# A hybrid decoder's decay rows: spread to all partitions by a transfer from memory in place of a TensorE product

## The chip, the cores and the metric

The kernel runs on one core of one Trainium2 chip. The metric is the device time of one execution in microseconds (us). The core has TensorE (PE), VectorE (DVE), ScalarE (ACT), GpSimd (POOL) and SyncE (SP, which here only starts transfers), and 16 DMA engines.

## The reference, cut to what matters

Two layers of a decoder trunk on 512 tokens of 1,024 channels. Each layer runs a state-space mixer (Mamba-2) and a differential attention mixer side by side, merges them by gates, and adds a squared-ReLU MLP. The part around the change is the state-space mixer with 32 heads of width 64, in 4 groups of 8 heads, over 4 chunks of 128 tokens:

```python
a_step = (dt * a)                       # per token and head
a_cum = jnp.cumsum(a_step, axis=2)      # running sums within a chunk
seg = a_cum[:, :, :, None] - a_cum[:, :, None, :]
decay = jnp.exp(jnp.where(causal, seg, -jnp.inf))
cb = jnp.einsum("bclgn,bcsgn->bclsg", Cc, Bc)
y_diag = jnp.einsum("bclsgr,bcsgrp->bclgrp", cb[..., None] * decay, X)
chunk_decay = jnp.exp(a_cum[:, :, -1])
```

For each head and chunk the kernel needs a 128 x 128 matrix with differences of the running sums: one token index lies over the partitions, the other along the row. The sum of the row's token has to be the same on all 128 partitions.

## The kernel before

All large products (projections, MLP) are made of units of 1,024 x 256 weights. Each weight is split into a high part in fp32r (`w_hi`, written by ACT, L930) and the rest (`w_lo`, written by GpSimd, L1796), and each product is three: high by high, high by low, low by high (L553 to L555 with 512 tokens as columns; L576 to L578, `unit_tokens`, with 256 columns). Raw weights are loaded by SyncE (L434) into two slots; a load waits until GpSimd is done with the slot, a conversion until PE is done with it, PE until GpSimd has written the low part (`lo_ready`).

The order of everything else is written out in ticks, from -10 to 59 for the state-space part and its surroundings in each layer. In each tick PE first does 2 to 6 parts of the running projection (`fill`; `SSD_FILL`), and then the small products of the tick. All engines go through the same ticks, each in its own order, and meet at semaphores. For tick t in 0 to 31:

- PE: `spread(t + 2)` (L721) takes one column of the selection matrix `sel`, broadcast over 128 columns as the weights, against `acum`, 64 rows by 512 columns, and so puts the running sums of head t + 2 on all partitions of a PSUM bank (banks 2 and 3 in turn). `acum` and `sel` are fp32r with 64 rows, since each sum is kept as a high part (rows 0 to 31) and the rest (rows 32 to 63). Then `diagonal(t)` (L734) multiplies the four 128 x 128 matrices `seg` of head t with `xdt`, in plain f32: eight instructions of 64 columns. Its end raises `m_used`. After it come chunk states (L745), off-diagonal products (L750), C by B (L758) and transposes (L618), as the tick has them.
- ACT: `decay(t + 1)` waits for the bank and for `m_used` of head t - 1, since `seg` has two buffers. Four activations (L1033, one per chunk, 128x128) compute relu(token's sum - row's sum) from PSUM into `seg`; after a drain one activation (L1037) takes the exponential of all four in place. Then ACT copies transposes out of PSUM (L1043, L1047), converts weights (L930), and starts and ends convolutions (L1011, L1017).
- DVE: `masked(t + 1)` (L1471) multiplies `seg` with the masked C by B.
- POOL: low parts of weights, and once a group of heads the tiles `xdt`, `xd` and the skip term.

Ahead of that, at tick -6, DVE makes `acum` out of PE's running sums (`decays_of_rows`, L1427 on), and `dcd`, which holds the chunks' last sums on a diagonal. PE sums `dcd` over its rows with a column of ones at tick -4 (`chunk_ends`, L770). The ticks' 32 heads in two layers make 64 calls of `spread`, at ticks -2 to 29.

Of the kernel before, what the change touches and what calls it, by code (L numbers as in the profile page):

```python
# [13 lines left out]
P = 128  # L14
# [77 lines left out]
LATE = [(0, m) for m in range(18, 24)] + [(1, m) for m in range(ADA)]  # L92
N_FIRST, N_EARLY, N_LATE = len(FIRST), len(EARLY), len(LATE)
N_LATE_AO = 2
ADA_G2 = LATE.index((0, ADA - 1))
EARLY_BUFS = 3
EARLY_AT = [37 + c for c in range(7)] + [44 + c // 2 for c in range(4 * N_EARLY - 7)]
# [48 lines left out]

BANK_KEYS = [[], [], [], []]
for _tick in range(T_FIRST, T_ATT):
    if 0 <= _tick + 2 < T_POST:
        BANK_KEYS[2 + _tick % 2].append(("sp", _tick + 2))  # L150
    if 0 <= _tick < T_POST and _tick % 2 == 0:
        BANK_KEYS[1].append(("d", _tick // 2))
    if step_at_tick(_tick):
        BANK_KEYS[0].append(step_at_tick(_tick))
    for _b, _key in EXTRA.get(_tick, ()):
        BANK_KEYS[_b].append(_key)
# [53 lines left out]
def build(nc, stream, dtw, params, consts, ropes, xT, xsave, out):  # L210
    ctx = ExitStack()
    with ctx:
        at = [nc.sbuf_base + (-nc.sbuf_base) % 32]

        ctx.enter_context(nc.sbuf_tensor("arena", [P, 212000 // 4], F32))

        def place(name, shape, dt, offset):
            return nc.alloc_sbuf_tensor_at(name, shape, dt, offset=offset)

# [37 lines left out]

        b_tok = place("b_tok", [P, TB, STATE], F32, r_op)
        cbm = place("cbm", [P, TB, P], F32, r_op + T2)
        seg = place("seg", [P, 2, TB, P], F32, r_op + 2 * T2)  # L260
        xdt = place("xdt", [P, TB, GW], F32, r_op + 4 * T2)
        xd = place("xd", [P, TB - 1, GW], F32, r_op + 8 * T2)
        state = place("state", [P, 2, GW], F32, r_op + 11 * T2)
        y_off = place("y_off", [P, GW], F32, r_op + 13 * T2)
        dcd = place("dcd", [2 * HEADS, HEADS, TB], F32R, r_op + 14 * T2)


        conv = place("conv", [P, 4, S], F32, r_g)
# [47 lines left out]
        def small(name, cols, dt=F32, rows=P):  # L316
            return place(name, [rows, cols], dt, region(cols * 4))
# [11 lines left out]
        lamw = small("lamw", 2 * AD)  # L329
        odd = small("odd", 8)  # L330
        lams, a_neg, subg = odd[:, 0:4], odd[:, 4:6], odd[:, 6:7]
        acum = small("acum", S, F32R, 2 * HEADS)
        sel = small("sel", HEADS + 2, F32R, 2 * HEADS)
        tok = place("tok", [P, TB, 3 * HEADS], F32, region(TB * 3 * HEADS * 4))
        ea_tok = place("ea_tok", [P, TB, HEADS], F32, region(TB * HEADS * 4))
        cdec = place("cdec", [P, HEADS, TB], F32, region(HEADS * TB * 4))
# [27 lines left out]
        con_in, par_in, dtw_in, x_in = sem("con_in"), sem("par_in"), sem("dtw_in"), sem("x_in")  # L364
        x_saved, x_back, rope_in, out_done = sem("x_saved"), sem("x_back"), sem("rope_in"), sem("out_done")
        ready = sem("ready")
        c_tanh, sel_ready = sem("c_tanh"), sem("sel_ready")
        S_ = {name: sem("s_" + name) for name in TOTAL if not name.startswith("bank")}

        LO_CREDIT, DONE_CREDIT, BANK_CREDIT, AUX_CREDIT, LAYER_CREDIT = 0, 4, 2, 1, 1  # L370
# [150 lines left out]
        def pe_program(pe):  # L521
# [115 lines left out]
            for l in range(DEPTH):  # L637
# [5 lines left out]
                if l == 0:  # L643
                    for n in range(2):
                        pe.wait_ge(pe_in[n], 16)
                        ada_piece(ada_pe[n], ab[3], 2 * FIRST_PE[n][1])
                    ada_column(0, ada_acc, ab[3], 2 * FIRST[0][1], 2, N_FIRST)
                    norm_sum(st)
                    pe.wait_ge(pe_in[2], 16)
                    ada_piece(ada_pe[2], ab[3], 2 * FIRST_PE[2][1])  # L650
                    norm_spread(st)
                    for n in range(1, N_FIRST):
                        ada_column(n, ada_acc, ab[3], 2 * FIRST[n][1], 2, N_FIRST)
                    pe.drain().then_inc(ada_full, 1)
                    pe.wait_ge(sel_ready, 1)
                else:

                    pe.wait_ge(ada_read, 6)
# [56 lines left out]
                last.then_inc(aux_full[2], 1)  # L715
                mid_part(KB - 1)

                def spread(r):

                    b = take(l, ("sp", r))  # L720
                    mm(b[:], sel[:, r:r + 1].broadcast_to([2 * HEADS, P]), acum[:], start=True, stop=True)\  # L721
                        .then_inc(give(("sp", r)), 1)

                def diagonal(r):

                    g = r // HG
                    b = ab[1]
                    if r % 2 == 0:
                        take(l, ("d", r // 2))
                    if r % HG == 0:  # L730
                        pe.wait_ge(S_["xdt"], mid_at(l, "xdt", g) + 1)
                    pe.wait_ge(S_["m"], mid_at(l, "m", r) + 1)
                    for t in range(TB):
                        last = mm(b[:, t * P + (r % 2) * HD:t * P + (r % 2 + 1) * HD], seg[:, r % 2, t, :],  # L734
                                  xdt[:, t, r % HG * HD:(r % HG + 1) * HD], start=True, stop=True)
                    last.then_inc(S_["m_used"], 1)
                    if r % 2:
                        pe.drain().then_inc(aux_full[1], 1)
# [28 lines left out]
                def chunk_ends():  # L767

                    b = take(l, ("cd",))
                    mm(b[:, 0:HEADS * TB], sel[:, HEADS:HEADS + 1].broadcast_to([2 * HEADS, P]),  # L770
                       dcd[:].rearrange("p h t -> p (h t)"), start=True, stop=True).then_inc(give(("cd",)), 1)

                def turn_x(n, j):
# [25 lines left out]
                for tick in range(T_FIRST, T_ATT):  # L799
                    if tick == T_FIRST + 2:  # L800
                        at = fill(at, 2)
                        x_to_tokens()
                        at = fill(at, 2)
                    elif tick > T_FIRST + 2:
                        at = fill(at, fill_of(tick))
                    if tick == T_FIRST + 3:
                        sums_of_dt()
                    if tick == T_FIRST + 5:
                        dt_to_tokens()
                    if 0 <= tick + 2 < T_POST:  # L810
                        spread(tick + 2)
                    if 0 <= tick < T_POST:
                        diagonal(tick)
                    step = step_at_tick(tick)
                    if step:
                        acts[step[0]](*step[1:])
                    for _, key in EXTRA.get(tick, ()):
                        acts[key[0]](*key[1:])
                    early(tick)
# [101 lines left out]
        def act_program(act):  # L921
# [47 lines left out]

            act.wait_ge(con_in, 16)  # L970
            A(cact[:, KB:2 * KB], con[:, K_C:K_C + KB], ACT.Tanh, scale=0.5).then_inc(c_tanh, 1)
            A(sel[:, 0:HEADS], con[0:2 * HEADS, K_SEL:K_SEL + HEADS], ACT.Copy)
            act.wait_ge(ready, 1)
            A(sel[:, HEADS:HEADS + 2], ones[0:2 * HEADS, 0:2], ACT.Copy).then_inc(sel_ready, 1)
            act.wait_ge(x_in, 16)
            squares_of_x(Step(0, "start"), range(KB), False)
            for l in range(DEPTH):
# [41 lines left out]
                def tokens_of_dt():  # L1019
# [4 lines left out]
                    A(ea_tok[:], tok[:, :, HEADS:2 * HEADS], ACT.Exp)  # L1024
                    A(tok[:, :, 2 * HEADS:3 * HEADS], tok[:, :, 2 * HEADS:3 * HEADS], ACT.Exp).then_inc(S_["dt_a"], 1)

                def decay(r):

                    b = full(l, ("sp", r))
                    if r >= 2:  # L1030
                        act.wait_ge(S_["m_used"], mid_at(l, "m_used", r - 2) + 1)
                    for t in range(TB):
                        last = A(seg[:, r % 2, t, :], b[:, t * P:(t + 1) * P], ACT.Relu, scale=-1.0,  # L1033
                                 bias=tok[:, t, HEADS + r:HEADS + r + 1])
                    last.then_inc(free(("sp", r)), 1)
                    act.drain()
                    A(seg[:, r % 2], seg[:, r % 2], ACT.Exp, scale=-1.0).then_inc(S_["decay"], 1)  # L1037

                def take_x(n, j):
                    g, u = divmod(n, 3)  # L1040
# [72 lines left out]
                for tick in range(T_FIRST, T_ATT):  # L1113
                    if 0 <= tick + 1 < T_POST:
                        decay(tick + 1)
                    for _, key in EXTRA.get(tick - 1, ()):
                        if l and key == ("x", 7, 0):
                            act.wait_ge(x_saved, 16)
                        if key[0] != "cb":
                            takes[key[0]](*key[1:])  # L1120
# [9 lines left out]
                        exp_of_dt()  # L1130
                    if tick == T_FIRST + 6:
                        tokens_of_dt()
                    for j in range(2):
                        for n in since(tick, U_Z, U_O, 1 + j):
                            tanh_z(n, j)
# [120 lines left out]
        def dve_program(dve):  # L1256
# [122 lines left out]
            for l in range(DEPTH):  # L1379
# [47 lines left out]
                def decays_of_rows():  # L1427
# [1 line left out]
                    dve.wait_ge(aux_full[2], st.at("bank2", 1) + 1)  # L1429
                    TS(dt_rows[0:HEADS], ab[2][0:HEADS, :], a_neg[0:HEADS, 1:2], None, ALU.mult).then_inc(aux_free[2], 1)  # L1430
                    settle()
                    v.tensor_copy(acum[0:HEADS], dt_rows[0:HEADS])
                    for t in range(TB):
                        c = slice(t * P, (t + 1) * P)
                        TS(dt_rows[HEADS:2 * HEADS, c], dt_rows[0:HEADS, c], -1.0,
                           dt_rows[0:HEADS, (t + 1) * P - 1:(t + 1) * P], ALU.mult, ALU.add)
                    settle()
                    TT(acum[HEADS:2 * HEADS], dt_rows[0:HEADS], acum[0:HEADS].bitcast(F32), ALU.subtract)
                    settle()
                    TT(dcd[:], con[0:2 * HEADS, K_SEL:K_SEL + HEADS].unsqueeze(2).broadcast_to([2 * HEADS, HEADS, TB]),  # L1440
                       acum[:, P - 1:S:P].bitcast(F32).unsqueeze(1).broadcast_to([2 * HEADS, HEADS, TB]), ALU.mult)
                    dve.drain().then_inc(S_["dt_v"], 1)

                def taps(n, j):
# [23 lines left out]
                def masked(r):  # L1468

                    dve.wait_ge(S_["decay"], mid_at(l, "decay", r) + 1)  # L1470
                    TT(seg[:, r % 2], seg[:, r % 2], cbm[:], ALU.mult).then_inc(S_["m"], 1)  # L1471

                def y_diag(d):

# [513 lines left out]
```

## Time and profile before

| | before |
|---|---|
| median of 3 runs | 2455.37 us |
| lowest, highest | 2454.77, 2455.37 us |
| profiled execution | 2454.4 us |
| its span, first to last instruction | 2452.6 us |
| instructions | 32,138 |
| busy: PE, DVE, ACT, POOL | 96%, 56%, 41%, 45% |
| moved by DMA | 250.27 MB |

The span is what the hardware profiler saw between the first and the last instruction. Busy shares are over the whole span; a stage can look quite different. In a timeline, the start of a group and the start of the next one tell what it costs on TensorE, because matmuls overlap: a duration there is longer than the distance to the next start. In this kernel's trace the names say "f32" for fp32r tiles of matmuls too.

### The profile page before, as it was taken

The page shows a single profiled execution, that of the slowest core. Times are in us where ns is not written, and L with a number is a line of the kernel's source. Part 1 is how long each engine was busy: PE and PEld are TensorE (multiplying, and loading weights), DVE is VectorE, ACT ScalarE, POOL GpSimd, SP SyncE. Part 2 cuts the span into 40 slices and gives each one's busy share as a digit, 9 for nine tenths or more (in the row PEclk, how much of TensorE's full clock was granted, in tenths as well). Part 3 has the DMA queues.
Part 4 walks back from the last instruction along what each step waited for, and adds up shares of the span by engine and source line. Part 5 has one row for each costly group of instructions (what it writes and reads, how often), then busy time and mean ns, then how long its engine had stood idle before and what let it go on. Part 6 is the DMA issues. An engine that isn't in the chain of part 4 may idle for free.

```text
span 2452.6 us, 32138 instructions
## 1 busy us (share of the span) xinstructions
PE 2350.7 (96%) x11862; PEld 1936.7 (79%) x11862; DVE 1379.8 (56%) x2043; ACT 998.7 (41%) x1864; POOL 1101.3 (45%) x825
## 2 busy tenths in 40 slices
PE   7999998999999989999989999999999998999997
PEld 6777897877778868888877778988777786888886
DVE  6666665556663657877757665632666533422323
ACT  2455553255554332322334555543555432322322
POOL 1365543533444434544434655454343444444542
PEclk9999999999999989999989999999999999999998
DMA  6211223622122435455422121232212232223221
GB/s 248 82 55 52 65 86 126 198 78 67 63 69 91 156 120 195 174 188 197 155 90 74 55 68 59 70 103 95 67 63 69 69 127 87 78 96 101 97 95 52
DMA packets 84812, 250.27 MB, mean 102 GB/s; under 512 B 7472, under 2 KB 34480, under 8 KB 79280
## 3 DMA queue, kind: packets, MB, share of 16 engines
q1 hardware_dynamic: 84656, 248.22, 29.9%
q8 instruction: 94, 1.54, 0.3%
q14 instruction: 62, 0.51, 0.1%
HBM read 244.00 MB, written 4.19 MB: 101 GB/s over the span
## 4 chain that ended last, share of the span: by engine, by line
issue 37%; PE 27%; POOL 16%; POOLq 14%; DVE 2%; DMA 1%; ACT 1%; PEld 1%; ACTq 1%; DVEq 0%; SPq 0%; PEldq 0%
POOL w_lo L1796 15%; POOLq L1798 14%; PE gemm L553 4%; PE gemm L555 4%; PE gemm L554 4%; PE aux L734 3%; PE gemm L576 2%; PE gemm L577 2%; PE gemm L578 2%; PE aux L618 1%; PE aux L721 1%; PE aux L745 1%; PE aux L750 1%; POOL smalls L1784 1%; DMA ada_pe<-stream 1%
## 5 line engine op out<-in xcount | busy, mean ns | idle before, releaser
L1796 POOL TENSOR_TENSOR w_lo<-raw,w_hi 128x512 fp32r<-128x512 f32 x704 | 975.8, 1407 | 1246.4 <-ACT w_hi L930 1238.8
L930 ACT ACTIVATE w_hi<-raw 128x1024 fp32r<-128x1024 f32 x352 | 371.0, 1057 | 688.4 <-PE gemm L555 623.5
L553 PE MATMUL gemm<-h_hi,w_hi 128*128 128x512 f32 x1504 | 607.8, 404 | 5.5 <-DVE h_lo L1360 4.9
L555 PE MATMUL gemm<-h_hi,w_lo 128*128 128x512 f32 x1504 | 593.7, 395 | 0.0
L554 PE MATMUL gemm<-h_lo,w_hi 128*128 128x512 f32 x1504 | 593.4, 395 | 0.0
L553 PEld LDWEIGHTS gemm<-h_hi,w_hi 128*128 128x128 f32 x1504 | 287.6, 191 | 66.9 <-issue 10.1
L555 PEld LDWEIGHTS gemm<-h_hi,w_lo 128*128 128x128 f32 x1504 | 286.8, 191 | 62.6
L554 PEld LDWEIGHTS gemm<-h_lo,w_hi 128*128 128x128 f32 x1504 | 287.4, 191 | 58.9 <-issue 1.9
L553 PE MATMUL gemm<-op_hi,w_hi 128*128 128x512 f32 x608 | 238.5, 392 | 0.2
L555 PE MATMUL gemm<-op_hi,w_lo 128*128 128x512 f32 x608 | 236.8, 390 | 0.0
L554 PE MATMUL gemm<-op_lo,w_hi 128*128 128x512 f32 x608 | 236.6, 389 | 0.0
L576 PE MATMUL gemm<-w_hi,h_hi 128*128 128x256 f32 x768 | 224.5, 292 | 2.2 <-ACT zh L1066 2.2
L577 PE MATMUL gemm<-w_hi,h_lo 128*128 128x256 f32 x768 | 217.2, 283 | 0.0
L578 PE MATMUL gemm<-w_lo,h_hi 128*128 128x256 f32 x768 | 217.1, 283 | 0.0
L1329 DVE SCALAR_TENSOR_TENSOR late_acc<-ada_late,first,late_acc 128x256 f32<-128x256 f32 x210 | 158.8, 756 | 7.5
L1033 ACT ACTIVATE seg<-aux,tok 128x128 f32<-128x128 f32 x256 | 73.0, 368 | 195.4 <-PE aux L734 184.6
L576 PEld LDWEIGHTS gemm<-w_hi,h_hi 128*128 128x128 f32 x768 | 147.2, 192 | 5.1 <-issue 4.9
L577 PEld LDWEIGHTS gemm<-w_hi,h_lo 128*128 128x128 f32 x768 | 147.2, 192 | 2.6 <-issue 2.4
L1744 DVE TENSOR_TENSOR usq<-relu 128x512 f32<-128x512 f32 x64 | 66.1, 1033 | 146.3 <-ACTq L1252 143.4
L578 PEld LDWEIGHTS gemm<-w_lo,h_hi 128*128 128x128 f32 x768 | 147.0, 191 | 0.0
L1451 DVE SCALAR_TENSOR_TENSOR conv<-gemm,cw,conv 128x511 f32<-128x511 f32 x144 | 107.8, 748 | 52.7 <-ACT conv L1011 41.4
L1764 DVE SCALAR_TENSOR_TENSOR x<-gemm,ada,x 128x512 f32<-128x512 f32 x64 | 45.9, 748 | 162.5 <-PE gemm L555 154.5
(196 smaller groups left out, 3421.6 us busy)
## 6 DMA issues: line engine op xcount, KB each, us to landing
raw<-stream SPq DMA_DIRECT2D x336, 512.0 KB
ada_late<-stream SPq DMA_DIRECT2D x30, 1024.0 KB, 4.8
ada_early<-stream SPq DMA_DIRECT2D x40, 256.0 KB, 3.9
raw<-stream SPq DMA_DIRECT2D x32, 256.0 KB
ada_first<-stream SPq DMA_DIRECT2D x5, 1024.0 KB, 20.1
x<-xT SPq DMA_DIRECT2D x2, 2048.0 KB, 10.4
ada_pe<-stream SPq DMA_DIRECT2D x3, 1024.0 KB, 14.1
xsave<-x SPq DMA_DIRECT2D x1, 2048.0 KB, 7.3
```

What stands on the lines that cost most here:

```text
L553: mm(o, w_hi[:, slot, k, cols], hi[:, k, :], start=k == 0, stop=False)
L554: mm(o, w_hi[:, slot, k, cols], lo[:, k, :], start=False, stop=False)
L555: last = mm(o, w_lo[:, slot, k, cols], hi[:, k, :], start=False, stop=k == KB - 1)
L576: mm(o, h_hi[:, k, toks], w_hi[:, slot, k, :], start=k == 0 and t % 2 == 0, stop=False, skip_group_check=True)
L577: mm(o, h_lo[:, k, toks], w_hi[:, slot, k, :], start=False, stop=False, skip_group_check=True)
L578: last = mm(o, h_hi[:, k, toks], w_lo[:, slot, k, :], start=False, stop=k == KB - 1, skip_group_check=True)
L734: last = mm(b[:, t * P + (r % 2) * HD:t * P + (r % 2 + 1) * HD], seg[:, r % 2, t, :], xdt[:, t, r % HG * HD:(r % HG + 1) * HD], start=True ...
L930: A(w_hi[:, slot, ks], raw[:, slot, ks], ACT.Copy).then_inc(hi_ready, 1)
L1329: STT(acc[:, n % ways], where[:, k], cact[:, k:k + 1], acc[:, n % ways], ALU.mult, ALU.add)\
L1451: last = STT(conv[:, c, lag:S], gb[c][:, 0:S - lag], cw[:, w:w + 1], conv[:, c, lag:S], ALU.mult, ALU.add)
L1796: gp.tensor_tensor(w_lo[:, slot, ks], raw[:, slot, ks], w_hi[:, slot, ks].bitcast(F32), ALU.subtract)
L1798: pool.drain().then_inc(lo_ready, 1)
```

## The change

The row of running sums of each head no longer comes from a product. ACT stores `acum` (now plain f32, 32 rows by 512) to a tensor `decay_rows` in memory once per layer, and for each head it starts a transfer that reads the head's 2 KB row 128 times, into all partitions of the `seg` buffer. `decay` then works in place, from SBUF. `seg` has three buffers in place of two, each with its own semaphore. `sel` and the low rows of `acum` go; `dcd` has 32 rows of f32, and the weights of `chunk_ends` are a column of `ones`.

```diff
+SEGS = 3
-    if 0 <= _tick + 2 < T_POST:
-        BANK_KEYS[2 + _tick % 2].append(("sp", _tick + 2))
+        rows = nc.dram_tensor("decay_rows", [DEPTH, HEADS, S], F32, kind="Internal").ap()
-        seg = place("seg", [P, 2, TB, P], F32, r_op + 2 * T2)
+        seg = place("seg", [P, SEGS, TB, P], F32, r_op + 2 * T2)
...
-        dcd = place("dcd", [2 * HEADS, HEADS, TB], F32R, r_op + 14 * T2)
+        dcd = place("dcd", [HEADS, HEADS, TB], F32, r_op + 15 * T2)
...
-        acum = small("acum", S, F32R, 2 * HEADS)
-        sel = small("sel", HEADS + 2, F32R, 2 * HEADS)
+        acum = small("acum", S, F32, HEADS)
...
-                def spread(r):
-
-                    b = take(l, ("sp", r))
-                    mm(b[:], sel[:, r:r + 1].broadcast_to([2 * HEADS, P]), acum[:], start=True, stop=True)\
-                        .then_inc(give(("sp", r)), 1)
...
-                    mm(b[:, 0:HEADS * TB], sel[:, HEADS:HEADS + 1].broadcast_to([2 * HEADS, P]),
+                    mm(b[:, 0:HEADS * TB], ones[0:HEADS, 0:1].broadcast_to([HEADS, P]),
...
-                    if 0 <= tick + 2 < T_POST:
-                        spread(tick + 2)
...
+                def rows_to_memory():
+
+                    act.dma_start(rows[l], acum[:]).then_inc(rows_out, 16)
+
+                def fetch_row(r):
+
+                    act.wait_ge(rows_out, (l + 1) * 16)
+                    if r >= SEGS:
+                        act.wait_ge(S_["m_used"], mid_at(l, "m_used", r - SEGS) + 1)
+                    act.dma_start(seg[:, r % SEGS].rearrange("p t n -> p (t n)"),
+                                  rows[l, r:r + 1, :].broadcast_to([P, S])).then_inc(seg_in[r % SEGS], 16)
+
                 def decay(r):
 
-                    b = full(l, ("sp", r))
-                    if r >= 2:
-                        act.wait_ge(S_["m_used"], mid_at(l, "m_used", r - 2) + 1)
+                    act.wait_ge(seg_in[r % SEGS], (l * len(range(r % SEGS, HEADS, SEGS)) + r // SEGS + 1) * 16)
                     for t in range(TB):
-                        last = A(seg[:, r % 2, t, :], b[:, t * P:(t + 1) * P], ACT.Relu, scale=-1.0,
-                                 bias=tok[:, t, HEADS + r:HEADS + r + 1])
-                    last.then_inc(free(("sp", r)), 1)
+                        A(seg[:, r % SEGS, t, :], seg[:, r % SEGS, t, :], ACT.Relu, scale=-1.0,
+                          bias=tok[:, t, HEADS + r:HEADS + r + 1])
                     act.drain()
-                    A(seg[:, r % 2], seg[:, r % 2], ACT.Exp, scale=-1.0).then_inc(S_["decay"], 1)
+                    A(seg[:, r % SEGS], seg[:, r % SEGS], ACT.Exp, scale=-1.0).then_inc(S_["decay"], 1)
...
                     if 0 <= tick + 1 < T_POST:
                         decay(tick + 1)
+                    if 0 <= tick + 2 < T_POST:
+                        fetch_row(tick + 2)
...
                         tokens_of_dt()
+                        rows_to_memory()
...
-                    v.tensor_copy(acum[0:HEADS], dt_rows[0:HEADS])
+                    v.tensor_copy(acum[:], dt_rows[0:HEADS])
...
-                    TT(acum[HEADS:2 * HEADS], dt_rows[0:HEADS], acum[0:HEADS].bitcast(F32), ALU.subtract)
-                    settle()
```

The store (`rows_to_memory`) is issued at tick -4, the first fetch at tick -2. ACT's two copies into `sel` at the kernel's start, and PE's wait for them, go as well.

## Rows read from the trace of the kernel before

**Rows 1.** The page, part 1: busy us (share of the span), instructions.

```profile
PE 2350.7 (96%) x11862; PEld 1936.7 (79%) x11862; DVE 1379.8 (56%) x2043; ACT 998.7 (41%) x1864; POOL 1101.3 (45%) x825
```

**Rows 2.** Table of stretches, state-space part of both layers: busy us, PEclk, DMA share, GB/s.

```profile
110.00:345.00 235.00, 230.96 (x1330) 186.51 (x1329) 157.50 (x195) 127.69 (x277) 124.48 (x100) 1.00 0.18 60
1328.00:1564.00 236.00, 231.93 (x1336) 187.37 (x1335) 157.14 (x195) 128.37 (x278) 124.99 (x100) 1.00 0.18 60
```

**Rows 3.** Waits from 110 to 345 us: us in total, times, longest.

```profile
ACT seg L1033 <- PE aux L734: 92.4, 29, 7.7
```

**Rows 4.** Line L721, the spread: ns min/median/max, first and last start.

```profile
L721 PE MATMUL aux<-acum,sel x64: 497/497/498, 113.2 to 1546.1; 64*128 64x512 f32 x64
```

**Rows 5.** Timeline of PE, 152 to 161 us: start us, us, instructions.

```profile
152.70 0.39 PE L555 MATMUL gemm<-h_hi,w_lo 128*128 128x512 f32 x1
153.02 0.50 PE L721 MATMUL aux<-acum,sel 64*128 64x512 f32 x1
153.44 1.10 PE L734 MATMUL aux<-xdt,seg 128*128 128x64 f32 x8
...
160.38 1.10 PE L734 MATMUL aux<-xdt,seg 128*128 128x64 f32 x8
```

**Rows 6.** Timeline of PE around 100 us.

```profile
99.79 0.39 PE L555 MATMUL gemm<-h_hi,w_lo 128*128 128x512 f32 x1
100.02 1.05 PE L758 MATMUL aux<-bct 128*128 128x128 f32 x8
101.00 0.32 PE L770 MATMUL aux<-dcd,sel 64*128 64x128 f32 x1
```

**Rows 7.** Timeline of PE around 327 us.

```profile
327.24 0.28 PE L578 MATMUL gemm<-w_lo,h_hi 128*128 128x256 f32 x1
327.45 0.50 PE L721 MATMUL aux<-acum,sel 64*128 64x512 f32 x1
327.88 1.10 PE L734 MATMUL aux<-xdt,seg 128*128 128x64 f32 x8
```

**Rows 8.** Timeline of PE around 333 us, in a tick without a spread.

```profile
333.24 0.28 PE L578 MATMUL gemm<-w_lo,h_hi 128*128 128x256 f32 x1
333.37 1.00 PE L734 MATMUL aux<-xdt,seg 128*128 128x64 f32 x8
```

**Rows 9.** Lines L1043 (from PSUM) and L1037 (from SBUF): ns min/median/max.

```profile
L1043 ACT ACTIVATE y_tok<-aux x32: 574/580/599, 101.9 to 1492.3; 128x512 f32<-128x512 f32 x32
...
L1037 ACT ACTIVATE seg<-seg x64: 631/632/635, 115.0 to 1549.0; 128x512 f32<-128x512 f32 x64
```

**Rows 10.** Timeline of ACT, 154 to 159 us.

```profile
154.65 1.14 ACT L1033 ACTIVATE seg<-aux,tok 128x128 f32<-128x128 f32 x4 [2.61 <-PE aux L734]
...
156.41 0.58 ACT L1043 ACTIVATE y_tok<-aux 128x512 f32<-128x512 f32 x1
156.89 1.05 ACT L930 ACTIVATE w_hi<-raw 128x1024 fp32r<-128x1024 f32 x1
157.83 1.44 ACT L1011 ACTIVATE conv<-gemm,cw 128x512 f32<-128x512 f32 x2
```

**Rows 11.** Line L482, 256 KB from memory: ns of the issue, us to landing.

```profile
L482 SPq DMA_DIRECT2D rope_cos<-ropes x2: 333/370/408, 406.9 to 1608.6; - x2
...
DMA to landing us min/median/max: 2.6/4.1/5.7
```

**Rows 12.** Line L734, 183 to 240 us: nine ticks, and who waited for it.

```profile
L734 PE MATMUL aux<-xdt,seg x72: 275/275/323, 184.2 to 239.8; 128*128 128x64 f32 x72
...
ACT seg L1033: 31.4, 9
```

**Rows 13.** DMA issues of the page: KB each, median us to landing.

```profile
out<-y_out SPq DMA_DIRECT2D x8, 256.0 KB, 2.7
```

**Rows 14.** Timeline of DVE, 151 us: the mask of the diagonal at 160.38.

```profile
151.51 0.69 DVE L1471 TENSOR_TENSOR seg<-seg,cbm 128x512 f32<-128x512 f32 x1
```

**Rows 15.** Cores: span and mean granted clock of TensorE.

```profile
core 0: 2452.6 us, clock 0.980
```

More of the change, by code:

```diff
@@ L259, in build @@
         cbm = place("cbm", [P, TB, P], F32, r_op + T2)
-        seg = place("seg", [P, 2, TB, P], F32, r_op + 2 * T2)
[L261 to L264, printed above, removed]
-        dcd = place("dcd", [2 * HEADS, HEADS, TB], F32R, r_op + 14 * T2)
+        seg = place("seg", [P, SEGS, TB, P], F32, r_op + 2 * T2)
+        xdt = place("xdt", [P, TB, GW], F32, r_op + 5 * T2)
+        xd = place("xd", [P, TB - 1, GW], F32, r_op + 9 * T2)
+        state = place("state", [P, 2, GW], F32, r_op + 12 * T2)
+        y_off = place("y_off", [P, GW], F32, r_op + 14 * T2)
+        dcd = place("dcd", [HEADS, HEADS, TB], F32, r_op + 15 * T2)
         conv = place("conv", [P, 4, S], F32, r_g)
@@ L366, in build @@
         ready = sem("ready")
-        c_tanh, sel_ready = sem("c_tanh"), sem("sel_ready")
+        c_tanh = sem("c_tanh")
+        rows_out, seg_in = sem("rows_out"), [sem(f"seg_in{n}") for n in range(SEGS)]
         S_ = {name: sem("s_" + name) for name in TOTAL if not name.startswith("bank")}
@@ L654, in pe_program @@
                     pe.drain().then_inc(ada_full, 1)
-                    pe.wait_ge(sel_ready, 1)
                 else:
@@ L733, in diagonal @@
                     for t in range(TB):
-                        last = mm(b[:, t * P + (r % 2) * HD:t * P + (r % 2 + 1) * HD], seg[:, r % 2, t, :],
+                        last = mm(b[:, t * P + (r % 2) * HD:t * P + (r % 2 + 1) * HD], seg[:, r % SEGS, t, :],
                                   xdt[:, t, r % HG * HD:(r % HG + 1) * HD], start=True, stop=True)
@@ L971, in act_program @@
             A(cact[:, KB:2 * KB], con[:, K_C:K_C + KB], ACT.Tanh, scale=0.5).then_inc(c_tanh, 1)
-            A(sel[:, 0:HEADS], con[0:2 * HEADS, K_SEL:K_SEL + HEADS], ACT.Copy)
             act.wait_ge(ready, 1)
-            A(sel[:, HEADS:HEADS + 2], ones[0:2 * HEADS, 0:2], ACT.Copy).then_inc(sel_ready, 1)
             act.wait_ge(x_in, 16)
@@ L1437, in decays_of_rows @@
                     settle()
-                    TT(acum[HEADS:2 * HEADS], dt_rows[0:HEADS], acum[0:HEADS].bitcast(F32), ALU.subtract)
-                    settle()
-                    TT(dcd[:], con[0:2 * HEADS, K_SEL:K_SEL + HEADS].unsqueeze(2).broadcast_to([2 * HEADS, HEADS, TB]),
-                       acum[:, P - 1:S:P].bitcast(F32).unsqueeze(1).broadcast_to([2 * HEADS, HEADS, TB]), ALU.mult)
+                    TT(dcd[:], con[0:HEADS, K_SEL:K_SEL + HEADS].unsqueeze(2).broadcast_to([HEADS, HEADS, TB]),
+                       acum[:, P - 1:S:P].unsqueeze(1).broadcast_to([HEADS, HEADS, TB]), ALU.mult)
                     dve.drain().then_inc(S_["dt_v"], 1)
@@ L1470, in masked @@
                     dve.wait_ge(S_["decay"], mid_at(l, "decay", r) + 1)
-                    TT(seg[:, r % 2], seg[:, r % 2], cbm[:], ALU.mult).then_inc(S_["m"], 1)
+                    TT(seg[:, r % SEGS], seg[:, r % SEGS], cbm[:], ALU.mult).then_inc(S_["m"], 1)
                 def y_diag(d):
```

## The prediction

> **What bounds the kernel now.** I read the engine shares of the page first: TensorE (PE) is busy 96% of the span [rows 1], so what PE is spared counts unless a wait takes its place. Then the stretch table, for the state-space part of each layer, the only place where the change acts: 231.0 of 235.0 us and 231.9 of 236.0 us PE-busy, at a granted clock of 1.00, with the DMA engines 18% in use [rows 2]. So PE sets the time there and the others follow it: the table of waits has ScalarE (ACT) waiting 92.4 us in 29 waits in this stretch for the diagonal products, L734 [rows 3]. Once a tick ACT is released by PE, does its work, and idles. The clock needs no step of its own in these stretches.
>
> **What is removed from PE.** L721 runs 64 times, 32 heads in two layers [rows 4]. Its own 497 ns is not its price, since matmuls overlap; I take the starts. After a 512-column product: L555 at 152.70, L721 at 153.02, L734 at 153.44, together 0.74 us [rows 5]. Without L721, L734 should follow as L758, a product in plain f32 from 128 rows like L734, follows L555: 99.79 to 100.02, 0.23 us [rows 6]. Saved 0.51. After a 256-column product: 327.24, 327.45, 327.88, together 0.64 us [rows 7]. The last two ticks of the part have no spread any more, and there the trace shows the very order that the change makes: L578 at 333.24, L734 at 333.37, 0.13 us (0.12 to 0.13 by rounding) [rows 8]. Saved 0.51 to 0.52. So both kinds give the same, and 64 x 0.515 = 33.0 us. It is more than twice the 0.23 us at which 512-column products follow each other in [rows 5]: a 64-row product between 128-row ones costs 0.09 us at its head and 0.20 us at its tail besides. The lower bound is that only the 0.23 goes: 14.7 us.
>
> **What is added to PE.** The chunk-end product (L770) goes from 64 to 32 rows and from fp32r to f32, which takes two instructions. Twice in the run; the one of now starts at 101.00 and is 0.32 long [rows 6]. L758 spends 1.05 us on eight instructions of this width [rows 6], so one more is about 0.1 us: 0.2 us in all, 0 to 0.6 as bounds (the other end is a second one at full length for each). Net 33.0 - 0.2 = 32.8 us.
>
> **ACT's work per row.** The relus read SBUF and not PSUM. The trace has no 128x128 relu from SBUF; the nearest rows are 128x512 ones, 580 ns from PSUM and 632 ns from SBUF [rows 9]: some 50 ns each, 0.2 us for four, bounds 0 and 0.3. The decay block takes 154.65 to 156.41 = 1.76 us now [rows 10], so 2.0 us. The DMA issue is new on ACT: SyncE's issues of a 256 KB load from memory take 333 to 408 ns [rows 11]. I take 0.4 us, within ACT's idle time: 31.4 us in 9 waits, 3.5 us a tick [rows 12]. That idle time is the cover of all of this. If it were gone, 0.6 us x 64 = 38 us would be the bill. There is one store of 64 KB per layer too; the first fetch comes two ticks behind it, longer than any landing below.
>
> **The wait that is added.** ACT now does, in each tick t: decay(t+1), which waits for the landing of its row; the fetch of row t+2, which waits for the diagonal t-1; then copies, conversions of weights, convolution work. Before, the wait for the diagonal stood ahead of decay, at the same diagonal. Behind a late landing stand decay, the next fetch, and ACT's conversions (GpSimd waits for these, PE for GpSimd) and bank evictions. How late may it be? Nine diagonals start from 184.2 to 239.8, and the last start belongs to the eighth product of the ninth block, 0.8 us in: 54.8/8 = 6.85 us a tick, and 6.34 after the change [rows 12]. The loop is landing + 2.0 us of decay (the issue lies within the landing time, the rest of ACT's work lies beside it: from 156.41 to about 159.3 in [rows 10], 2.9 us, no longer than a landing). So the landing may average 6.34 - 2.0 = 4.3 us.
>
> The nearest rows: 256 KB from memory to 128 partitions, 2 KB each, landed in 2.6 us in one layer and 5.7 us in the other, where the queue had weight loads ahead of it [rows 11]; 256 KB to memory in 2.7 us [rows 13]. With the engines 18% in use [rows 2], and 16.8 MB more over the two stretches (64 x 256 KB), most rows should land like the free one and a few like the late one. I take 2.6 + 0.2 x 3.1 = 3.2 us, bounds 2.6 and 5.7. No row of this trace shows 128 reads of the same 2 KB.
>
> The Trainium skill (DMA: Bandwidth & Descriptors, Latency and other measured facts) speaks against such a source: copies whose 128 partition streams lie 4 MiB apart ran at 103 GB/s where others ran at 207, and the page puts it, as an inference, to streams in step on one memory channel. One row read 128 times would be the extreme of that. By it, an estimate, 256 KB need 2.5 us and not 1.3, and the landing is 4.4 and not 3.2 us: the loop would just miss its tick, and 58 x 0.1 = 6 us would be lost.
>
> **A single late row costs PE nothing.** The mask for a diagonal now ends at 152.2 for a diagonal that starts at 160.38 [rows 5, 14]: 8.2 us ahead. With three buffers the fetch of row r starts behind diagonal r-3, three ticks (19 us) before its own. Landing 5.7, decay 2.0 and a mask of 0.7 still leave 10 us. Only a mean above 4.3 us adds up.
>
> **VectorE** loses a 32-partition subtraction per layer, ahead of the part, not on PE's path: 0. SBUF addresses move: 0. Weight loads share engines with the new 256 KB; the loads are a unit ahead, so 0; if they had no lead, PE would wait up to 3.1 us (5.7 - 2.6) at each load that meets a fetch.
>
> **Sum.** The profiled execution took 2454.4 us, its span of 2452.6 and 1.8 around it. 2454.4 - 32.8 = 2421.6 us. The median of the runs is 1.0 above it, so 2422.6 us. A measurement of this kernel can tell about 0.2%, 5 us, from no change.
>
> **The rivals.**
> - *Forecast, PE is spared 0.51 us a head and nothing waits*, 0.70. Its own range is 2416 to 2428: the term's rounding and the chunk ends are 1 us; the mean clock is 0.980 [rows 15], so 4% of the span, 98 us, ran at half rate in other stages, and if a tenth of it falls otherwise when all comes 33 us earlier, that is 5 us of time.
> - *The switch cost stays*: L734 behind a 512-column product still pays at its head, so only 14.7 us go: 2440.7 us. [rows 8] speaks against it, but only for 256-column neighbours; for the others I borrow L758. 0.06.
> - *Landings a little long*, a mean of 4.3 to 4.9 us: each 0.1 us above 4.3 costs 58 x 0.1 = 5.8 us (58 fetches wait for a buffer), so 2422 to 2455 us, with 2440 in the middle. 0.08. For it: nothing here shows a repeated source. The rule of the Trainium skill's page named above (DMA: Bandwidth & Descriptors) would end here.
> - *PE had cover that the trace does not show*: the freed time goes to waits for ACT, VectorE or GpSimd, which now have 7% less time per tick. 2450 to 2458 us. Against it: the waits run toward PE [rows 3]. 0.04.
> - *The landing becomes the bound* (the other side): at a mean of 5.7 us the loop is 7.7 us, 1.36 above the tick, 58 x 1.36 = 79 us lost against 33 won: 2501 us. It decides from 6.34 + 33/58 - 2.0 = 4.9 us, and is slower by more than 0.2% from 5.0 us. For it: the one late landing [rows 11]. Against it: three like transfers near 2.7, and idle DMA engines. 0.12.
>
> **How the numbers follow.** Faster by over 0.2%: 0.70 + 0.06 + 0.07 of the third = 0.83. Within: 0.01 + 0.04 = 0.05. Slower: 0.12. The range of 2416 to 2446 us takes in the forecast's, the switch rival and the lower two thirds of the third case, 0.8.
>
> **What would show it.** L721 gone and L734 0.23 or 0.12 us behind the last gemm product, also in ticks that had a spread; diagonals 6.34 us apart; PE as busy as now in both stretches, each some 16 us shorter; the seg fetches landing at about 3 us; ACT's waits before seg split between the landing and L734's release, with masks no later before their diagonals. Wrong would be: a DMA as what PE's, GpSimd's or VectorE's waits lead back to, or landings above 4.3 us in the mean; or L734 still 0.4 us behind its forerunner.

## The result, and the profile after

The changed kernel took 2408.6 us in the median of 4 runs (2407.1 to 2409.8) against 2455.4 us, a ratio of 0.9816 with an interval of 0.9801 to 0.9831. That is 46.8 us faster, where the forecast had 32.8 us and a range that ended at 2416 us. The direction and what bounds the kernel were as forecast. The price of the product was not.

The cores and the page of the changed kernel, then its table of stretches for the same part of both layers (the answers to [rows 15], [rows 1] and [rows 2]):

```profile
core 0: 2406.6 us, clock 0.981
```

```profile
PE 2307.6 (96%) x11800; PEld 1924.0 (80%) x11800; DVE 1376.5 (57%) x2041; ACT 1012.4 (42%) x1862; POOL 1106.4 (46%) x825
...
q10 hardware_dynamic: 9312, 16.91, 2.5%
...
seg<-decay_rows ACTq DMA_DIRECT2D x64, 256.0 KB, 3.4
```

```profile
110.00:330.00 220.00, 216.27 (x1348) 186.84 (x1347) 160.96 (x198) 135.51 (x277) 127.70 (x101) 1.00 0.33 102
1300.00:1520.00 220.00, 216.89 (x1337) 186.66 (x1336) 159.25 (x197) 137.03 (x280) 127.33 (x100) 1.00 0.34 105
```

PE is 98% busy in the part, as before. The DMA engines' share rose from 0.18 to 0.33 and 0.34, and a second queue (q10, ScalarE's) moved the 16.9 MB. Landings have a median of 3.4 us, where the prediction took 3.2.

The timeline of PE around the diagonal that answers to [rows 5], and the line of the diagonals over nine ticks, to be read against [rows 12]:

```profile
147.88 1.00 PE L728 MATMUL aux<-xdt,seg 128*128 128x64 f32 x8
148.72 1.08 PE L744 MATMUL aux<-state,bct 128*128 128x512 f32 x2
...
153.97 0.39 PE L556 MATMUL gemm<-h_hi,w_lo 128*128 128x512 f32 x1
154.19 0.55 PE L728 MATMUL aux<-xdt,seg 128*128 128x64 f32 x4
```

```profile
L728 PE MATMUL aux<-xdt,seg x72: 217/275/275, 176.2 to 226.7; 128*128 128x64 f32 x72
```

The diagonal (now L728) starts 0.22 us behind the last gemm product: the forecast's 0.23. But the block is also shorter. It is 1.00 us long, not 1.10. Nine blocks lie between 176.2 and 226.7 us; by the reckoning of the prediction that is (50.5 - 0.7)/8 = 6.23 us a tick against 6.85. So 0.62 us a head went, not 0.515. That is a mean: in the changed kernel the diagonals start between 4.9 and 10.8 us apart, and before it was 5.5 to 11.4.

ScalarE's timeline in the same tick, and its main waits from 110 to 330 us (the answers to [rows 10] and [rows 3]; ACTq is its queue of instructions):

```profile
146.79 1.28 ACT L1033 ACTIVATE seg<-seg,tok 128x128 f32<-128x128 f32 x4
148.14 0.63 ACT L1036 ACTIVATE seg<-seg 128x512 f32<-128x512 f32 x1
148.97 0.33 ACTq L1026 DMA_DIRECT2D seg<-decay_rows  x1
150.27 0.60 ACT L1042 ACTIVATE y_tok<-aux 128x512 f32<-128x512 f32 x1 [1.50 <-PE aux L619]
150.76 1.05 ACT L922 ACTIVATE w_hi<-raw 128x1024 fp32r<-128x1024 f32 x1
151.71 1.44 ACT L1001 ACTIVATE conv<-gemm,cw 128x512 f32<-128x512 f32 x2
153.04 1.27 ACT L1033 ACTIVATE seg<-seg,tok 128x128 f32<-128x128 f32 x4
```

```profile
ACT w_hi L922 <- PE aux L728: 26.4, 9, 5.8
ACT seg L1033 <- DMA seg<-decay_rows: 16.2, 21, 2.8
```

A fetch is issued at 148.97, behind the end of the diagonal that freed its buffer. The decay at 153.04 belongs to that row, 4.1 us later, and starts as soon as the convolution's work is done. Decay takes 2.0 us (146.79 to 148.77), as estimated. ScalarE does wait for landings, 16.2 us in 21 waits. That PE does not feel them is what e5 tests below.

### The profile page after: what moved, and what is told of

Its sections match the earlier page's. It is cut to its first block, busy times and chain, and to the rows that moved or that the text cites. A ratio compares the mean times of both kernels' runs of the same rounds, so it can differ in the third digit from the quotient of the medians.

```text
span 2406.6 us, 32072 instructions
## 1 busy us (share of the span) xinstructions
PE 2307.6 (96%) x11800; PEld 1924.0 (80%) x11800; DVE 1376.5 (57%) x2041; ACT 1012.4 (42%) x1862; POOL 1106.4 (46%) x825
## 4 chain that ended last, share of the span: by engine, by line
issue 38%; PE 25%; POOL 16%; POOLq 14%; DVE 2%; DMA 1%; PEld 1%; ACT 1%; DVEq 1%; ACTq 0%; SPq 0%; PEldq 0%
POOL w_lo L1796 15%; POOLq L1798 14%; PE gemm L554 4%; PE gemm L556 4%; PE gemm L555 4%; PE gemm L577 2%; PE gemm L578 2%; PE gemm L579 2%; PE aux L728 2%; PE aux L619 1%; PE aux L739 1%; PE aux L744 1%; POOL smalls L1784 1%; DMA ada_pe<-stream 1%; PEld aux L606 1%
## 5 line engine op out<-in xcount | busy, mean ns | idle before, releaser
L556 PEld LDWEIGHTS gemm<-op_hi,w_lo 128*128 128x128 f32 x608 | 114.1, 188 | 24.2
```

What stands on the lines that cost most here:

```text
L556: last = mm(o, w_lo[:, slot, k, cols], hi[:, k, :], start=False, stop=k == KB - 1)
```

## Experiments

All runs below are set beside the kernel before on their own chip; its median there was 2451.4, 2451.2 and 2452.8 us in the three groups (e1 to e4, e5 to e8, e9 to e12). Differences to the changed kernel are against the 2408.1 us of its own second measurement (e10), which was made on the chip of e9 to e12. The kernel before was 1.4 and 1.6 us faster on the chips of the other two groups, so a difference of e1 to e8 to the changed kernel may be that much too low.

**Is it the product, and which part of it?** The first four runs put an idle product back into the changed kernel, at the spread's old place and into its old bank. ScalarE's decay waits for it and frees the bank, as before the change. The lines on TensorE's side:

```diff
+                def spread(r):
+                    b = take(l, ("sp", r))
+                    last = mm(b[:], h_hi[0:64, 0, 0:P], h_hi[0:64, 0, :], start=True, stop=True)   # e1; e3: twice
+                    last = mm(b[:], h_hi[:, 0, 0:P], h_hi[:, 0, :], start=True, stop=True)         # e2
+                    last = mm(b[:, 0:P], h_hi[0:64, 0, 0:P], h_hi[0:64, 0, 0:P], start=True, stop=True)   # e4
+                    last.then_inc(give(("sp", r)), 1)
...
+                    if 0 <= tick + 2 < T_POST:
+                        spread(tick + 2)
```

- e1: 

> The changed kernel, with an idle product put back on TensorE where the spread was: 64 rows by 512 columns, fp32r, into the old bank; nobody uses its result, ScalarE only frees the bank. Theory A (the price is that of a 64-row product between 128-row ones, start to start, plus what it does to the diagonal block behind it): 0.62 us for each of 64, so 39 us slower than the changed kernel, about 2448 us, 0.997 of the kernel before; the block L734 is 1.10 us long again and not 1.00. Theory B (the forecast's 0.515 us was right and the rest of the gain came from elsewhere in the loop of ScalarE and the banks): 33 us, about 2441 us. Theory C (the price was that of waits, not of the product): under 15 us more than the changed kernel, 2408 to 2423 us.


- e2: 

> The same idle product with all 128 rows: 128 rows by 512 columns, fp32r. Theory A (the change between 64 and 128 rows costs 0.39 us, the columns 0.23): 64 x 0.23 = 15 us over the changed kernel, about 2423 us, and L734 stays 1.00 us long. Theory D (any product of another kind put there costs 0.6 us, rows do not matter): 39 us, 2448 us.


- e3: 

> Two idle 64-row products, one directly behind the other, 512 columns each. Theory A (the price beyond the columns is paid where the number of rows changes, once on the way in and once on the way out): 39 + 15 = 54 us over the changed kernel, about 2463 us. Theory E (each 64-row product pays it by itself): 78 us, about 2487 us.


- e4: 

> The idle 64-row product with 128 columns and not 512. Theory A (a fixed price of the change of rows, beside 0.23 us for 512 columns): 0.62 less three quarters of 0.23, so 0.45 us each, 29 us over the changed kernel, about 2437 us. Theory F (the price grows with the columns, since the next weights load only behind them): a quarter of 39 us, 10 us, about 2418 us.

| run | product put back | median us | over the changed kernel | theory A |
|---|---|---|---|---|
| e1 | 64 rows, 512 columns | 2449.2 | 41.1 | 39 |
| e2 | 128 rows, 512 columns | 2423.8 | 15.8 | 15 |
| e3 | 64 rows, 512 columns, twice | 2464.3 | 56.2 | 54 |
| e4 | 64 rows, 128 columns | 2437.0 | 29.0 | 29 |

Theory A held in all four, to some 2 us (some 3 to 4 when each is set against the kernel before on its own chip); B, C, D, E and F fell. The timelines show where it sits. In e1:

```profile
151.97 0.39 PE L558 MATMUL gemm<-h_hi,w_lo 128*128 128x512 f32 x1
152.29 0.50 PE L723 MATMUL aux<-h_hi 64*128 64x512 f32 x1
152.71 1.10 PE L736 MATMUL aux<-xdt,seg 128*128 128x64 f32 x8
153.66 1.08 PE L752 MATMUL aux<-state,bct 128*128 128x512 f32 x2
```

In e2, with the same columns and all rows:

```profile
150.09 0.39 PE L558 MATMUL gemm<-h_hi,w_lo 128*128 128x512 f32 x1
150.32 0.39 PE L723 MATMUL aux<-h_hi 128*128 128x512 f32 x1
150.55 1.00 PE L736 MATMUL aux<-xdt,seg 128*128 128x64 f32 x8
151.38 1.08 PE L752 MATMUL aux<-state,bct 128*128 128x512 f32 x2
```

From the last gemm product to what follows the diagonal: 1.69 us in e1, 1.29 in e2. The 0.40 us lie in three places: 0.09 ahead of the idle product, 0.19 behind it, and 0.12 within the diagonal block. In e3:

```profile
154.21 0.73 PE L724 MATMUL aux<-h_hi 64*128 64x512 f32 x2
154.86 1.10 PE L737 MATMUL aux<-xdt,seg 128*128 128x64 f32 x8
```

From the first of the two 64-row products to the diagonal it is 0.65 us, which is e1's 0.42 and 0.23 more: inside the 64-row stretch a product costs its columns alone. e4 says the same of short ones: three quarters of the columns less is 12.1 us less for 64 (11.0 us by the 0.23), and the rest of the price stays.

The Trainium skill (TensorEngine Tiling (Array Packing), Key Properties under Tiling Modes) says that changing the tiling mode drains TensorE. The price of 0.40 us for going in and out fits that; that a lone 64-row product counts as such a mode, and that a drain is what the time goes to, no run here shows.

**e9, the kernel before with a padded product.** The same idea tested on the other side: the spread stays, over 128 rows, 64 of them zeros.

```diff
-        acum = small("acum", S, F32R, 2 * HEADS)
-        sel = small("sel", HEADS + 2, F32R, 2 * HEADS)
+        acum = small("acum", S, F32R)
+        sel = small("sel", HEADS + 2, F32R)
...
+            for h in range(2):
+                TS(acum[2 * HEADS:P, h * 256:(h + 1) * 256], con[2 * HEADS:P, 0:256], 0.0, None, ALU.mult)
...
-                    mm(b[:], sel[:, r:r + 1].broadcast_to([2 * HEADS, P]), acum[:], start=True, stop=True)\
+                    mm(b[:], sel[:, r:r + 1].broadcast_to([P, P]), acum[:], start=True, stop=True)\
```

> The kernel before, with its spread kept, but over 128 rows: sel, acum and dcd get 64 more rows of zeros. No transfer, no third buffer. Theory A (0.39 of the 0.62 us is the change of row count): 64 x 0.39 = 25 us under the kernel before, 0.990, about 2427 us. Rival (part of the price lies in the waits for the banks or in the order of the kernel before): under 10 us.

It took 2426.8 us (ratio 0.9895, 0.9880 to 0.9910): 26.1 us under the kernel before, against 25 expected. More than half of the change's gain is to be had without any transfer. The spread in its timeline:

```profile
149.65 0.39 PE L555 MATMUL gemm<-h_hi,w_lo 128*128 128x512 f32 x1
149.88 0.39 PE L721 MATMUL aux<-acum,sel 128*128 128x512 f32 x1
150.11 1.00 PE L734 MATMUL aux<-xdt,seg 128*128 128x64 f32 x8
```

**e10, the changed kernel again.** 

> The changed kernel once more, on the chip of the others of this call. 0.98 of the kernel before. Theory A accounts for 39.4 us of the difference by the products; what is left beyond it should differ between profiled executions by which stretches ran at half clock.

2408.1 us (2405.0 to 2409.9), ratio 0.9816 (0.9802 to 0.9831), and the same mean clock, 0.981. It served as the base of the comparisons; by itself it does not settle which stretches ran at the lower clock by chance.

**e5, no fetches.**

```diff
-                    act.dma_start(seg[:, r % SEGS].rearrange("p t n -> p (t n)"),
-                                  rows[l, r:r + 1, :].broadcast_to([P, S])).then_inc(seg_in[r % SEGS], 16)
...
-                        A(seg[:, r % SEGS, t, :], seg[:, r % SEGS, t, :], ACT.Relu, scale=-1.0,
+                        A(seg[:, r % SEGS, t, :], bct[:, GROUPS, t * P:(t + 1) * P], ACT.Relu, scale=-1.0,
```

> The changed kernel without the 64 fetches and without the waits for their landing: the relus read another tile in SBUF, of the same shape, in place of the head's row, so the decays are of other numbers. It shows what the landing costs as it is, with ScalarE's order kept. Theory A (the landing of 3.4 us lies beside ScalarE's other work and PE's lead): same as the changed kernel, 2408.6 us within 5 us. Rival (some of the landing or its traffic is paid): 10 us or more below it, under 2399 us.

2407.4 us, 0.7 us from the changed kernel, and the same ratio to the kernel before (0.9817 and 0.9816): the landing and its traffic cost nothing that can be told from zero where they are.

**e8, another source.** `rows[l, r:r + 1, :].broadcast_to([P, S])` became `ropes[0]`. 

> The changed kernel with each fetch reading 128 different rows of 2 KB (the cosine table) and not one row 128 times, so the decays are of other numbers. Theory A (a repeated source costs nothing): the landing stays at a median of 3.4 us (3.0 to 4.7) and the time at 2408.6 us. Rival, after the rule on streams that meet in one memory channel: the landing falls toward the 2.6 us of the like load in the kernel before, by 0.5 us or more; the time stays, since the landing is hidden.

The fetch's line and landings, first in the changed kernel and then in e8:

```profile
L1026 ACTq DMA_DIRECT2D seg<-decay_rows x64: 326/326/376, 100.7 to 1495.0; - x64
...
DMA to landing us min/median/max: 3.0/3.4/4.7
```

```profile
L1026 ACTq DMA_DIRECT2D seg<-ropes x64: 334/334/392, 100.3 to 1497.2; - x64
...
DMA to landing us min/median/max: 2.5/2.7/5.2
```

One row read 128 times does land later, by 0.7 us in the median; the rival about the landing was right. The prediction's estimate of the price was 1.2 us (4.4 against 3.2). The two sources are different tensors as well, and what in memory makes the difference, one channel or another thing, this run does not show. The time was 2405.8 us, 2.3 us below, under what can be told.

**How far is the landing from being the bound?** Three runs moved or slowed it.

e7 fetches at the end of the tick, directly ahead of the next tick's decay. 

> The changed kernel with the fetch of row t + 2 as the last thing that ScalarE does in a tick, directly ahead of the decay that waits for a row. Forecast's loop account: other work of 2.0 to 2.9 us + landing 3.4 us + decay 2.2 us in one chain a tick if the fetch waits at that place for its own row, 7.6 to 8.5 us against 6.24: 1.4 to 2.3 us more for each of 58, 80 to 130 us over the changed kernel, 2490 to 2540 us. Rival (PE's lead and the three buffers absorb it, since the decay at the head of a tick is of a row that was fetched a tick before): under 10 us over, below 2419 us.

2421.5 us, 13.4 us over the changed kernel: between the two. ScalarE's waits from 110 to 330 us:

```profile
ACT seg L1033 <- DMA seg<-decay_rows: 71.3, 32, 4.1
```

That is 2.2 us a wait and one nearly every tick, where it was 16.2 us in 21. With the 132.3 us for which ScalarE is busy there, it is taken for 204 of 220 us. The account had added the landing in full, 3.2 us here, and took the other work at up to 2.9 us. ScalarE is busy 132.3 us in about 34 ticks, 3.9 us each with decay, so 1.9 us of other work. And the landing does not start behind that work:

```profile
146.44 0.33 ACTq L1026 DMA_DIRECT2D seg<-decay_rows  x1
147.25 1.05 ACT L922 ACTIVATE w_hi<-raw 128x1024 fp32r<-128x1024 f32 x1
```

The fetch stands behind this conversion in ScalarE's program and is issued 0.81 us ahead of its start, and the decay that waits for it starts at 149.52. So 1.9 + 2.0 + 2.2 us is 6.1, not 8. PE pays for it almost only in the last ticks of the part. Its busy time in e7 from 110 to 290 us is 176.9 us, against 177.5 in the changed kernel; behind that, in e7 and then in the changed kernel:

```profile
290.00:330.00 40.00, 34.01 (x255) 30.44 (x255) 29.30 (x37) 22.43 (x50) 18.67 (x14) 1.00 0.35 107
```

```profile
290.00:330.00 40.00, 38.73 (x303) 36.19 (x302) 29.72 (x39) 23.04 (x48) 16.32 (x13) 1.00 0.30 90
```

e11 put an idle transfer of 512 KB ahead of each fetch:

```diff
+                    if l or r:
+                        act.wait_ge(idle_in, (l * HEADS + r) * 16)
+                    act.dma_start(idle[:], ropes.rearrange("a p n -> p a n")).then_inc(idle_in, 16)
```

> The changed kernel with an idle transfer of 512 KB into unused SBUF put ahead of each fetch on ScalarE's queue, so that the fetch lands later, at about 5 us (3.4 us and some 1.7 us for the bytes ahead of it); ScalarE issues one transfer more a head, 0.33 us. Forecast's loop account with the landing measured (landing + 2.2 us of decay against a tick of 6.24 us, nothing lost below 4.0 us): at 5 us 1.0 us a head for 58, some 55 us over the changed kernel, 2460 us. Rival (issues and waits run ahead of the activations, and the bound lies higher): under 10 us over it.

2445.0 us (2439.0 to 2452.4), 37 us over. Its fetches:

```profile
L1031 ACTq DMA_DIRECT2D seg<-decay_rows x64: 326/491/1308, 101.4 to 1532.8; - x64
...
DMA to landing us min/median/max: 3.7/4.6/6.7
```

A median landing of 4.6 us, 1.2 us more than in the changed kernel, together with the second issue (the fetch's own now takes 491 ns in the median and up to 1308), brings PE down from 216.3 to 207.5 us busy of 220. By the loop account with 4.6 us, 0.6 us a head or 35 us should go, and 37 went. That agreement is luck. The account takes the same from every head, and the trace does not show that: PE loses in a few places. From 180 to 220 us, in e11 and then in the changed kernel:

```profile
180.00:220.00 40.00, 35.33 (x174) 28.42 (x173) 27.50 (x37) 23.77 (x48) 17.97 (x14) 0.94 0.57 184
```

```profile
180.00:220.00 40.00, 39.27 (x203) 31.38 (x202) 30.85 (x40) 27.18 (x55) 19.55 (x16) 1.00 0.38 125
```

In the 40 us behind that, e11's PE is busy 39.4 us against 39.5. No transfer of weights is among PE's waits from 110 to 330 us. The longest in total is for a copy of DVE:

```profile
PE aux L730 <- DVE y_tok L1486: 5.4, 2, 4.2
```

The one of 4.2 us ends at 215.78. DVE's mask had waited 4.05 us for the late decay, until 207.32, then came 4.93 us of convolution (from 209.97), and only then the copy (215.04). It is the chain that e12 shows below.

And the granted clock fell, from 1.00 in both stretches to 0.97 and 0.98. By mean clock and span (0.976 against 0.981), e11 ran some 26 us more at the lower clock, some 13 of the 37 us. The issues on ScalarE's queue grew in the same run too. So e11 shows that landings of 4.6 us with a second issue are no longer hidden; it does not show a threshold.

e6 uses two buffers, e12 three, both with the fetch first and decay last in ScalarE's tick:

```diff
-SEGS = 3
+SEGS = 2        # e6 alone
...
                     if 0 <= tick + 1 < T_POST:
-                        decay(tick + 1)
-                    if 0 <= tick + 2 < T_POST:
-                        fetch_row(tick + 2)
+                        fetch_row(tick + 1)
...
+                    if 0 <= tick + 1 < T_POST:
+                        decay(tick + 1)
```

e6: 

> The changed kernel with two buffers for seg and not three: in each tick ScalarE first fetches the row of head t + 1, then does the tick's other work, and the decay of t + 1 last. Forecast's account (landing 3.4 us beside 2 to 3 us of other work, then 2.2 us of decay, against a tick of 6.24 us, and PE 8 us behind the masks): 0 to 5 us over the changed kernel, 2409 to 2414 us. Rival (the third buffer is what hides the landing): at least 0.5 us a head lost, 32 us, 2440 us or more.

e12: 

> The order of the two-buffer run (fetch first, decay last in each tick) with three buffers. Theory G (that run lost its time since the mask on VectorE, which waits for the decay, holds back VectorE's copies and convolution work of the tick, not for want of a buffer): again about 2467 us. Rival (the missing buffer did it): 2409 us within 5.

e6 took 2467.0 us (1.0066, 1.0051 to 1.0081), slower than the kernel before. e12 took 2448.0 us. So neither side of e12 was right alone: the order (fetch first, decay last) costs 39.9 us and the missing buffer 19.0. Both hold some time at the lower clock: by mean clock (0.979 in e12, 0.975 in e6, 0.981 in the changed kernel) some 6 of the 39.9 us, and some 10 of the 19.0. DVE's timeline in e12 shows the first part:

```profile
158.21 0.69 DVE L1471 TENSOR_TENSOR seg<-seg,cbm 128x512 f32<-128x512 f32 x1 [3.74 <-ACT seg L1036]
158.82 4.93 DVE L1451 SCALAR_TENSOR_TENSOR conv<-gemm,cw,conv 128x511 f32<-128x511 f32 x6
163.88 0.69 DVE L1481 TENSOR_TENSOR y_tok<-y_tok,aux 128x512 f32<-128x512 f32 x1
```

The mask waits 3.74 us for a decay that PE does not need yet, and 4.93 us of convolution queue up behind it on DVE; then comes the copy that frees PE's bank. PE waits for that copy, and as long for other late work of DVE:

```profile
PE aux L619 <- DVE yn L1536: 4.9, 3, 2.3
PE aux L728 <- DVE y_tok L1481: 4.2, 3, 1.9
```

In the changed kernel PE waits 0.8 us for `yn` from 110 to 330 us, and not at all for the copy.

My expectation for e6 had counted PE's lead over the masks and not what stands behind the mask on DVE's own queue. The third buffer itself could not be taken out of the changed kernel in its own order: there the fetch of row t + 2 would wait, with two buffers, for a diagonal that waits for work behind it on ScalarE; that was not run.

## Why the prediction was off

- **PE bounds the part**: right. It is 98% busy before and after, and e5 shows that nothing of the landing is paid.
- **Start to start, 0.515 us a head**: right as far as it went. It took the distance from the last gemm product to the diagonal's start, and the diagonal starts 0.22 us behind it now.
- **"What is removed from PE", the sum of 33.0 us**: this is the term that failed. The mechanism, a 64-row product that goes from TensorE, was right, and the term was too small. It stopped at the diagonal's start. [rows 7] and [rows 8] already show that L734 takes 1.10 us behind a spread and 1.00 us without one, and I read only their first column. With it the price is 0.62 us a head, 64 x 0.62 = 39.7 us; e1 puts back 41.1 us, with e2 to e4 and e9 each within 2 us of what this price gives.
- **The rest.** 46.8 - 39.7 = 7 us against the first measurement, 44.8 - 39.7 = 5 us on the chip of e9 to e12. The trace shows where it lies. The diagonals of the two layers, before and then after:

```profile
L734 PE MATMUL aux<-xdt,seg x256: 221/275/323, 129.4 to 339.8; 128*128 128x64 f32 x128
L734 PE MATMUL aux<-xdt,seg x256: 221/275/323, 1348.0 to 1558.5; 128*128 128x64 f32 x128
```

```profile
L728 PE MATMUL aux<-xdt,seg x256: 217/275/275, 126.3 to 318.2; 128*128 128x64 f32 x128
L728 PE MATMUL aux<-xdt,seg x256: 217/275/275, 1320.9 to 1512.1; 128*128 128x64 f32 x128
```

They are 18.5 and 19.3 us shorter. Each holds 29 of the 32 products, 18.0 us at 0.62. So some 2 us of the rest fall within the two parts, and some 4 to 5 us of the two profiled executions outside them. The clock is one piece of that. By mean clock and span, before ran 2 x 0.020 x 2452.6 = 98 us at the lower of its two clocks (1.2 and not 2.4 GHz), after 2 x 0.019 x 2406.6 = 91 us, which is 3.5 us of time if PE was at work in it. I had allowed for 5 us of this kind. It accounts for nothing on the chip of e9 to e12: there the 19 runs of the kernel before have a mean clock of 0.982 in the median, the four of the changed kernel 0.981. The piece within the parts is a wait of PE that I had not looked for. The page's rows for the 256-column products, of before, of after, and of e1 (the last entry of each is PE's idle time ahead of them, and what ended it):

```profile
L576 PE MATMUL gemm<-w_hi,h_hi 128*128 128x256 f32 x768 | 224.5, 292 | 2.2 <-ACT zh L1066 2.2
```

```profile
L577 PE MATMUL gemm<-w_hi,h_hi 128*128 128x256 f32 x768 | 224.4, 292 | 0.0
```

```profile
L579 PE MATMUL gemm<-w_hi,h_hi 128*128 128x256 f32 x768 | 224.6, 292 | 0.3
```

Up to 2.2 us went because ScalarE's copies for the z gate no longer stand behind a decay that waits for a diagonal. In the kernel before, the decay at 296.45 us had waited 7.67 us for the diagonal, the copy behind it started at 299.64, and PE waited 1.10 us for it. e9, in the old order, still has them (2.2); e10 has 0.0, and e2, with a product put back, 0.7. And e1, which has both the product and the transfer, is 2.2 us faster than the kernel before (0.9995, 0.9984 to 1.0007), so what the change gives beside the product is of this size, and can't be told from nothing by time alone. Why fewer stretches ran at the lower clock in one execution, and what the last 3 us on the chip of e9 to e12 are, stays open; the interval of that ratio is wider than they are (0.9802 to 0.9831, 3.6 us to each side).
- **Chunk ends, SBUF relus, the issue**: the chunk ends went from 0.25 us to the next line's start (101.00 to 101.25) to 0.42 (99.44 to 99.86), 0.3 us in all where 0.2 was reckoned; the relu went from 368 to 388 ns, 20 ns and not 50; the issue takes 326 ns and not 400. All small.
- **The landing**: 3.4 us against 3.2, hidden: right. The account of what a longer one would cost failed. It set landing and decay against a mean tick of 6.34 us and took 58 x 0.1 us for each 0.1 us above 4.3. At e11's median of 4.6 us that is 17 us, and 37 went; with the fetch in the worst place (e7) 13 us went, where the same account said 80 to 130. Ticks are not equal. In one of 5.0 us a landing of 3.4 and a decay of 2.0 are already too long, and one of 10.4 us can make up for it. What PE pays is decided in single ticks, by what stands behind the late decay, and the mean tick does not tell it.
- **The range** of 2416 us at its low end held only what the forecast's own terms allowed. The upper side had four rivals; the lower had none, since nothing was asked of what else the product might slow. The measured price alone, 39.7 and not 33.0 us, gives 2415.9 us, just outside; the waits and the clock did the rest.

## What to carry to other kernels

Price a product on TensorE from the instruction ahead of it to the end of the block behind it, and compare with a tick that lacks it: a 64-row product among 128-row ones cost 0.62 us, of which 0.23 us were its columns. Padding its rows with zeros took 26 us off this kernel, with the spread left in its place. The transfer replaced it for nothing here, issued as soon as its buffer was free and with its consumer where the other engines' orders expect it; the order with fetch first and decay last cost 40 us, the landing nothing. And look at the ticks one by one before a mean is set against a latency: here they were 4.9 to 10.8 us.

## What the runs showed of the hardware

- A 64-row product between 128-row ones costs 0.39 to 0.40 us beside its columns (e1 against e2, e9): 0.09 us ahead of it, 0.19 behind it, and 0.10 to 0.12 us within the block of eight f32 instructions behind it. Two in a row pay it once (e3).
- Reading one 2 KB row of memory 128 times landed 0.7 us later (3.4 us in the median) than reading 128 rows of another tensor once each (2.7 us), 256 KB in both cases (e8).
- A load started by ScalarE takes 326 ns of its queue. Its issue does not wait for the activations that stand before it: in e7 it started 0.81 us ahead of one of them. With two loads in a row, the second's issue took 491 ns in the median and up to 1308 (e11).
